# Expert rows of two tiles scaled on ScalarE and summed by accumulating transposes on TensorE, none on VectorE

## The reference

```python
gate = jax.nn.softmax(top_s.astype(jnp.float32), axis=-1).astype(hc.dtype)
u = jnp.take(expert_u, experts, axis=0)
act = jax.nn.gelu(jnp.einsum('chkd,cd->chk', u, hc))
v = jnp.take(expert_v, experts, axis=0)
return jnp.einsum('chk,chkd->cd', gate * act, v)
...
x = x + gate2 * peer(h2, w_query[l], sub_keys_1[l], sub_keys_2[l], expert_u[l], expert_v[l])
return rmsnorm_2(x, final_g)
```

## Time and profile before

| what | value |
|---|---|
| median of three executions | 2421.08 us |
| span of the profiled execution | 2420.9 us |
| TensorE busy in the span | 2179.9 us (90%) |
| VectorE busy | 1680.5 us (69%) |
| ScalarE busy | 742.0 us (31%) |
| first and last gather issued at | 920.7 and 2393.9 us |
| bytes moved | 754.23 MB, of them 588.90 MB by the queue that holds the gathers |

### The profile page before, as it was taken

How to read it: one execution, slowest core, us unless ns; L and a number is a source line. 1 busy time by engine, 2 the same in 40 slices (tenths; PEclk the granted TensorE clock), 3 DMA queues, 4 the chain that set the end, 5 groups by cost and what they waited for, 6 DMA issues and landing times.

```text
span 2420.9 us, 25182 instructions
## 1 busy us (share of the span) xinstructions
PE 2179.9 (90%) x8180; PEld 1438.7 (59%) x8180; DVE 1680.5 (69%) x3748; ACT 742.0 (31%) x2094; POOL 636.1 (26%) x606
## 2 busy tenths in 40 slices
PE   7999998999999998999998999799988977877776
PEld 3444787788888886777774656565444423333332
DVE  5563645476657737889988998877666666676664
ACT  2321345421103212322324223244333333342322
POOL 2100000000110002333334334344444443444342
PEclk9999998999999999999999999899999999999999
DMA  8631020266774348999999999999999999999997
GB/s 344 200 121 54 35 70 1 106 233 222 261 276 146 130 161 322 390 416 398 400 417 419 419 400 384 399 391 420 421 420 421 421 421 421 415 422 421 421 415 306
DMA packets 131785, 754.23 MB, mean 312 GB/s; under 512 B 14544, under 2 KB 14672, under 8 KB 65616
## 3 DMA queue, kind: packets, MB, share of 16 engines
q0 software_dynamic: 87456, 588.90, 60.1%
q1 hardware_dynamic: 44208, 163.84, 18.6%
HBM read 750.59 MB, written 2.10 MB: 311 GB/s over the span
## 4 chain that ended last, share of the span: by engine, by line
PE 52%; DMA 28%; DVE 13%; ACT 4%; issue 2%; POOL 0%; DVEq 0%; SPq 0%; ACTq 0%; POOLq 0%
PE PS L601 51%; DMA arena<-experts_dram,ecur 23%; DVE arena L2605 4%; DVE arena L1874 3%; DMA ring<-down_dram 2%; DVE h_all L1874 2%; DMA ring<-up_dram 1%; ACT const L1756 1%; ACT L1748 1%; DMA ring<-query_dram 1%; ACT arena L1752 1%; DVE h_all L1868 1%; DMA ring<-branch_dram 1%; DVE arena L1868 1%; DMA xT<-x_dram 0%
## 5 line engine op out<-in xcount | busy, mean ns | idle before, releaser
L601 PE MATMUL PS<-arena,const 128*128 128x512 f32 (+2 forms) x1708 | 810.1, 619 | 176.6 <-ACT const L1756 169.8
L601 PE MATMUL PS<-h_all,ring 128*128 128x256 f32 (+2 forms) x3584 | 883.5, 404 | 16.4 <-DMA ring<-up_dram 5.1
L2780 POOL DMA_INDIRECT arena<-experts_dram,ecur x512 | 587.0, 1147 | 1100.1 <-PE PS L601 785.6
L2605 DVE CUSTOM_DVE_ANT_0 arena<-arena 128x1024 f32<-128x1024 f32 x512 | 625.9, 1223 | 278.2 <-DMA arena<-experts_dram,ecur 274.6
L601 PEld LDWEIGHTS PS<-h_all,ring 128*128 128x128 f32 x3584 | 678.9, 191 | 227.7 <-issue 130.8
L601 PEld LDWEIGHTS PS<-arena,const 128*128 128x128 f32 x1708 | 325.1, 197 | 594.1 <-issue 331.9
L1748 ACT ACTIVATE arena<-arena 128x2 f32<-128x2 f32 x255 | 51.6, 202 | 721.4 <-DVE arena L2605 721.0
L601 PE MATMUL PS<-arena,ring 128*128 128x256 f32 x1088 | 245.0, 384 | 7.3 <-DMA ring<-down_dram 4.5
L601 PEld LDWEIGHTS PS<-arena,ring 128*128 128x128 f32 x1088 | 206.4, 192 | 42.7 <-DMA ring<-down_dram 10.7
L601 PE MATMUL PS<-arena 128*128 128x128 f32 (+4 forms) x936 | 137.8, 299 | 8.5 <-DVE arena L1868 3.4
L1756 ACT ACTIVATE const<-const,arena 128x128 f32<-128x128 f32 x415 | 143.5, 387 | 0.0
(11 more groups left out here) (273 smaller groups left out, 1481.2 us busy)
## 6 DMA issues: line engine op xcount, KB each, us to landing
ring<-up_dram SPq DMA_DIRECT2D x88, 512.0 KB, 3.3
ring<-w_in_dram SPq DMA_DIRECT2D x80, 512.0 KB, 4.0
arena<-ada_dram POOLq DMA_DIRECT2D x80, 512.0 KB, 5.5
ring<-w_out_dram SPq DMA_DIRECT2D x32, 512.0 KB, 5.6
ring<-query_dram SPq DMA_DIRECT2D x32, 512.0 KB
ring<-down_dram SPq DMA_DIRECT2D x16, 704.0 KB, 6.3
ring<-branch_dram SPq DMA_DIRECT2D x16, 512.0 KB
arena<-experts_dram,ecur POOLq DMA_INDIRECT x512
```

Of the source, the lines that this page charges most:

```text
L601: return nc.tensor.matmul(o, l, r, start=start, stop=stop)
L2605: V.tensor_tensor_reduce(out=u, in0=u, in1=hrow[:, (r // HEADS) % 2, :], scale=1.0, scalar=0.0, op0=MUL, op1=ADD, accum_out=dots[:, p % NB ...
L2780: nc.gpsimd.indirect_dma_start(out=ring_e[:, g % RING, :], out_offset=None, in_=a["experts"], in_offset=bass.IndirectOffsetOnAxis(ap=ecur[ ...
```

## The change

All 256 rows of tiles 0 and 1 (`turned(p)`, p < 128) now take one other way. ScalarE makes no diagonal; it scales `v` itself in its slot, 1024 columns per row, with the weight as scale (`row_scaled`). TensorE then adds the row with eight transposes of 128 x 128 (`add_turned`) that accumulate into the same two PSUM banks, so that the sum of a tile stands there turned: features on the partitions. No row is summed on VectorE and `side`, `side_row` and `side_sum` are gone; the ring stays at nine slots. At the end of tiles 0 and 1, VectorE adds the turned sum, times the gate, to the turned residual `xT` (`add_tile`, eight instructions of 128 columns at pairs 67 and 131), and `turn_x` turns x with the sum in it, so `finish` drops its two sums of 1024 columns. Tiles 2 and 3 keep diagonals. Four semaphores of an early stage are merged into one, `gate_step`, that counts 1, 2, 3, 4 in the order of the four before.

```diff
-ONE = [*range(1, 48), *range(52, 61), *range(81, 100)]
-BOTH = [*range(4, 46, 4), 14, 18, 19, 22, 23, 30, 34, 38, 39]
-SIDE = sorted([2 * p + 1 for p in ONE] + [2 * p for p in BOTH])
+TURNED = 2
+def turned(p):
+    return p < TURNED * TILE
...
+            def add_turned(row, start, stop):
+                for k in range(KT):
+                    ins = nc.tensor.matmul(PS[:, k // 4, (k % 4) * P:(k % 4 + 1) * P], row[:, k * P:(k + 1) * P], ident,
+                                           start=start and k % 4 == 0, stop=stop and k % 4 == 3, is_transpose=True)
+                return ins
...
             def row_pair(p, start, stop):
-                for k in rows:
-                    r = (p * BATCH + k) % RING
+                for k in range(BATCH):
+                    g = p * BATCH + k
+                    r = g % RING
+                    if turned(p):
+                        pe.wait_ge(row_scaled, g + 1)
+                        add_turned(ring_e[:, r, D:], start and k == 0, stop and k == BATCH - 1).then_inc(rows_used, 1)
+                        continue
...
-            def side_sum(c):
-                pe.wait_ge(side_used, sides(BATCH * TILE * (c + 1)))
-                for v in range(2):
-                    mm(PS[:, v, :], ident, side[:, v * S:(v + 1) * S], False, False)
...
             def weigh_pair(p, r):
-                rows = tensor_rows(p)
-                for k in rows:
+                for k in range(BATCH):
                     act.wait_ge(w_ready2, BATCH * p + k + 1)
-                    A(diag[:, b, k, :], ident, ACT.Copy, scale=wts[:, b, k:k + 1]).then_inc(diag_ready if k == rows[-1] else act_step, 1)
+                    if turned(p):
+                        row = ring_e[:, (BATCH * p + k) % RING, D:]
+                        A(row, row, ACT.Copy, scale=wts[:, b, k:k + 1]).then_inc(row_scaled, 1)
+                    else:
+                        A(diag[:, b, k, :], ident, ACT.Copy, scale=wts[:, b, k:k + 1]).then_inc(diag_ready if k == BATCH - 1 else act_step, 1)
...
+            def add_tile(c):
+                dve.wait_ge(prow_ready, 2 * (c + 1))
+                for k in range(KT):
+                    x = xT[:, k, c * P:(c + 1) * P]
+                    stt(x, prow[:, k * P:(k + 1) * P], mod[:, 1, 40 + k:41 + k], x, MUL, ADD).then_inc(tile_added, 1)
...
                 for j in range(TOPK):
                     g = r * TOPK + j
                     old = g - RING
-                    if old >= 0 and old in SIDE:
-                        pool.wait_ge(side_used, sides(old + 1))
-                    elif old >= 0:
-                        pool.wait_ge(rows_used, by_tensor(old + 1))
+                    if old >= 0:
+                        pool.wait_ge(rows_used, old + 1)
```

More of the change, by code:

```diff
@@ L688, in gate_sums @@
             def gate_sums():
-                pe.wait_ge(g_ready, 1)
+                pe.wait_ge(gate_step, 1)
                 mm(PS[:, 4, 0:16], cst("upper"), gsm[:, 5, :])
-                mm(PS[:, 4, 16:32], ones, gsm[:, 5, :]).then_inc(gc_done, 1)
+                mm(PS[:, 4, 16:32], ones, gsm[:, 5, :]).then_inc(gate_step, 1)
             def decay(h):
@@ L1142, in turn_rows @@
                 ins.then_inc(hr_done, 1)
+            def add_turned(row, start, stop):
[3 more added lines that the diff above has]
+                return ins
             def row_pair(p, start, stop):
-                rows = tensor_rows(p)
-                if rows and p < LAST:
-                    pe.wait_ge(diag_ready, weighed(p + 1))
+                if p < LAST and not turned(p):
+                    pe.wait_ge(diag_ready, p - TURNED * TILE + 1)
                 if start:
@@ L2607, in row_dot @@
                                        ).then_inc(dots_ready, 1)
-            def side_row(g):
-                p, k = divmod(g, BATCH)
-                w = wts[:, p % NB, k:k + 1]
-                row = ring_e[:, g % RING, D:]
-                dve.wait_ge(w_ready2, g + 1)
-                if g == min(q for q in SIDE if q // (BATCH * TILE) == p // TILE):
-                    ts(side, row, w, None, MUL, ALU.bypass).then_inc(side_used, 1)
-                else:
-                    dve.wait_ge(side_used, n.now(side_used))
-                    stt(side, row, w, side, MUL, ADD).then_inc(side_used, 1)
-                n(side_used)
             def finish(c):
@@ L2627, in finish @@
                 dve.wait_ge(brow_ready, 4)
+                if c < TURNED:
+                    V.tensor_tensor_reduce(out=prow, in0=x, in1=x, scale=1.0, scalar=0.0,
+                                           op0=MUL, op1=ADD, accum_out=fin[:, 0:1]).then_inc(fin_sq, 1)
+                    n(fin_sq)
+                    return
                 tt(prow, prow, grow, MUL).then_inc(vec_step, 1)
@@ L2640, in scale_rows @@
                 dve.wait_ge(vec_step, n(vec_step))
-                stt(prow, prow, fin[:, 0:1], frow, MUL, MUL).then_inc(fin_ready, 1)
+                if c < TURNED:
+                    dve.wait_ge(fin_sq, n.now(fin_sq))
+                stt(prow, hrow[:, c % 2, :] if c < TURNED else prow, fin[:, 0:1], frow, MUL, MUL).then_inc(fin_ready, 1)
                 n(fin_ready)
@@ L2668, in beside @@
                 c, q = divmod(p, TILE)
-                for g in range(BATCH * (p - 1), BATCH * p):
-                    if g in SIDE:
-                        side_row(g)
                 for g in range(4):
@@ L2708, in beside @@
                         add_part(m)
+                if c and q == 3 and c <= TURNED:
+                    add_tile(c - 1)
                 if p in FIN_AT:
```

44 lines of the change are left out of this document (18 added, 26 removed).

## The result

| kernel | executions | median, us | range, us | ratio to before, 95% interval |
|---|---|---|---|---|
| before, beside the first runs of the changed one | 4 | 2419.40 | 2417.68 to 2421.54 | 1 |
| changed | 4 | 2433.16 | 2427.31 to 2434.85 | 1.0043 (1.0029 to 1.0057) |
| changed, once more, beside 23 of before (median 2422.07) | 6 | 2431.73 | 2430.79 to 2434.33 | 1.0045 (1.0029 to 1.0061) |

The changed kernel is slower, by 0.43 to 0.45%, some 10.5 us. The forecast was 2419 us and no change. The result is inside the range that was given, 2405 to 2436 us, but it is a loss, and it lies on the rival "TensorE's stalls stay", whose total of 2434 us is close, though, as the profile shows, not by its mechanism.

A forecast was written before the change was run, and what follows sets the result against it. DMA at 420 GB/s was taken as the bound, with TensorE last in pairs 0 to 47 and VectorE in 60 to 79. Terms +2 + 1 - 2.5 - 0.5, then -2, against 2420.9 gave 2419 us; range 2405 to 2436.

The forecast's parts named there:

- TensorE's stalls stay: Rival, pairs 0 to 47: 18 to 29 us of TensorE stalls remain, total about 2434 us; chance 0.22.
- What becomes of the stalls in pairs 0 to 47: Pairs 0 to 47: stalls shrink to 8 us, stretch takes 345 instead of 331 us; net charge 2 us.
- credit behind them, and VectorE's relief: Behind pair 47: DMA runs four or five rows ahead and TensorE catches up, absorbing 12 of the 14 us.
- pairs 64 to 71 with `add_tile`: Pairs 60 to 80: eight `add_tile` instructions, say 2.3 us, against at most one side row less (1.28 us): net +1 us.
- the rest to pair 99: Slots free on time in 1480 to 1500 us win 2.5 us, pair 100's shorter work 0.5 us.
- POOL's waits for side rows: POOL's ten slot waits, 27 us, end with the side rows; less than a tenth counted, -2 us.
- What bounds the kernel: Expert stage: DMA can do 420 GB/s, 29 us lost in all; TensorE comes last in 946 to 1277 us.
- TensorE's price: TensorE, per row: eight transposes at 0.11 us each, 0.88 us, instead of 1.72 us by diagonals.
- 1345 to 1480: Pairs 60 to 79 with the convolution: VectorE stays the limit, windows stay near 404 GB/s, 5 us lost stay.
- 1480 to 1500: Window after the convolution: DMA rises from 355 to over 400 GB/s, 2.5 of 3.1 us won.
- ScalarE: Scaling a row takes 1.15 us; ScalarE has room, at most one row's delay, 2.5 us, in total.
- Clock: Rival: transposes drop TensorE to 1.2 GHz for a tenth of pairs 0 to 47, 17 us more, 2434 us; chance 0.06.

The follow-up runs named there:

- tile 1 alone: Kernel before with only tile 1 changed to scaled rows and transposes; tile 0 keeps diagonals and its 76 side rows: 2421.83 us, ratio 1.0000.
- all side rows: Changed kernel, but VectorE keeps all 95 side rows of before, the other rows still turned on TensorE: 2415.82 us, ratio 0.9978.
- 47 side rows: Changed kernel, but VectorE keeps one side row per pair in pairs 1 to 47 and none behind: 2415.96 us, ratio 0.9963.
- half the transposes: Changed kernel with four of eight transposes per row in pairs 1 to 47, so its sum is incomplete: 2413.37 us, ratio 0.9956.
- 24 late ones: Changed kernel, but VectorE keeps 24 side rows, one per pair in pairs 24 to 47: 2426.91 us, ratio 1.0017.
- tile 0 alone: Kernel before with only tile 0 changed; tile 1 keeps diagonals and its 19 side rows: 2434.50 us, ratio 1.0054.
- scaled twice: Changed kernel with ScalarE scaling each row of pairs 0 to 47 twice, first into an unused buffer: 2432.99 us, ratio 1.0040.
- 24 early ones: Changed kernel, but VectorE keeps 24 side rows, one per pair in pairs 1 to 24: 2420.15 us, ratio 0.9990.
- diagonals only: All rows of tiles 0 and 1 by diagonals on TensorE, none summed on VectorE, none turned: 2520.61 us in one execution.

## Why the prediction was wrong

**The step that failed** is the one under "What becomes of the stalls in pairs 0 to 47": "I charge 14 - 12 = 2 us", with the reason that "the DMA, with time to spare, has nearly all nine landed at the same pair, four or five rows (10 to 12 us) further on". What is ahead of row 95 is bounded by the slots that TensorE frees: a gather whose slot comes free late is issued late, whatever time the transfers have to spare. At row 95, 100 gathers are issued in the changed kernel and 101 in the one before, and in both programs the landed rows end with row 95. The "several rows still to bring" of the prediction were there, but they were there before too, and no further on.

What does come back can be read from rows 95 to 127. With the nine side rows of pairs 52 to 60 this part takes 96.8 and 98.3 us (before), 97.7 (tile 1 alone) and 97.6 (all side rows). Without them, and with TensorE relieved up to row 95, it takes 95.2, 95.3 and 96.8 (47 side rows, half the transposes, 24 late ones): 1.8 less in the mean, which I put down to VectorE's relief. Without them and with TensorE late it takes 93.6 to 94.4 (changed twice, tile 0 alone, scaled twice, 24 early ones): 0.8 to 3.2 less again, 1.8 in the mean. That is the credit: 1 to 3 us where I had 12, and some 5 (90.7) with a TensorE that is 88 us late.

The sum as measured, for the two profiles of the changed kernel against each of the two of before:

| term | predicted, us | against the second profile of before | against the first |
|---|---|---|---|
| pairs 0 to 47 | +14 | +14.6 | +10.3 |
| credit behind them, and VectorE's relief | -12 | -4.6 | -3.1 |
| pairs 64 to 71 with `add_tile` | +1 | +1.8 | +1.8 |
| the rest to pair 99 | -3 | -0.2 to +1.2 | -1.5 to -0.1 |
| POOL's waits for side rows | -2 | not seen as a term | not seen as a term |
| behind pair 99 | 0 | +0.3 | +0.1 |
| sum | -2 | +11.9 to +13.3 | +7.6 to +9.0 |

The third line is rows 127 to 143: 54.3 us in the second profile of before (1368.1 to 1422.4), 56.1 in the second of the changed kernel (1379.0 to 1435.1). All nine profiles with tile 0 turned have 56.0 to 56.2 there, the four others 54.1 to 54.5, so `add_tile` costs nearly its own length. Its eight instructions in the changed kernel's first profile (group; busy, mean ns, idle before):

```profile
L1857 DVE SCALAR_TENSOR_TENSOR xT<-arena,mod,xT 128x128 f32<-128x128 f32 x8 | 2.2, 343 | 0.0
```

The ratio's 10.5 us lie between the two sums, which differ by what one execution of before differs from another. Against either, most of the 12 us is missing. The base of the forecast has a small slip besides: 2420.9 is a span, so it stands for a time of about 2422.6 us and the forecast for 2420.6; against an error of 12 us that is little.

**Point by point.** *What bounds the kernel*: right for 946 to 1277. The 420 GB/s hold in every kernel from 1766 us on (419 to 421). *TensorE's price*: right. The timeline of the changed kernel has sixteen transposes in 1.91 us, here between two weight blocks:

```profile
1003.58 1.91 PE L1127 MATMUL PS<-const,arena 128*128 128x128 f32 x16
```

With 337 us of work and little stall left but the start, the stretch of 344.4 is the predicted 345. *Stalls*: right that they go; TensorE's waits for weights are 0.9 us in the first profile and 1.4 in the second. The rival that kept 18 to 29 us of them is refuted, though its total came out.

*VectorE*: 212 us, as announced (215). *1345 to 1480*: 408 GB/s, near the 404 announced.

*1480 to 1500*: announced over 400, measured 382 and 390, where the two profiles of before have 355 and 372; that is 1 to 2 us (20 x 27/420 and 20 x 18/420) of the 2.5. By rows, 161 to 175 are 1.5 us shorter (first profiles) and 2.3 (second), and rows 175 to 199 are 0.1 us shorter and 3.5 longer, so in the second pair nothing of it is kept. With tile 1 alone the gain goes in the same place, where TensorE is busy 78 of 83 us.

*ScalarE*: its row took 1.134 us, and its length costs nothing; with the row made twice as dear it cost 1.3 us at row 95. The Trainium skill ("ScalarE: Activation LUTs", section "What ACT_TABLE_LOAD costs") gives 280 ns + 0.833 ns a column for an instruction with one operand read per partition. The trace agrees: an estimate of 1133 ns by that formula, 1134 measured.

*Clock*: right, 0.99 in pairs 0 to 47 with 711 transpose records among the matmuls. The clock fell in 1623 to 1766, where TensorE has mostly transposes. The windows of the second profiles of before and of the changed kernel, and of the one with tile 0 alone changed, which has diagonals there:

```profile
1623.00:1766.00 143.00, 131.94 (x396) 72.23 (x395) 98.33 (x250) 59.76 (x182) 56.04 (x53) 0.97 1.01 421
1623.00:1766.00 143.00, 108.49 (x654) 97.86 (x653) 97.82 (x240) 96.47 (x178) 66.12 (x56) 0.86 1.00 412
1623.00:1766.00 143.00, 134.98 (x432) 77.53 (x431) 96.52 (x238) 58.24 (x178) 59.90 (x53) 0.99 1.01 414
```

The first profile of the changed kernel has 0.84 there. The Trainium skill's rule that a transpose doesn't count as activity ("TensorE: Matmul & The Clock Gate", section "Part 4: PE-mode transpose") fits that. It isn't shown by it, because TensorE is also busy for less of the time, 108 us instead of 132; with diagonals and 48 of 60 us busy, in 1480 to 1540, the kernel before had 0.89. No kernel here is seen to have lost time by the clock.

**What the change was.** Two halves that nearly cancel: 95 rows given from VectorE to TensorE cost some 98 us at diagonal prices (one execution of 2520.61 us beside 2422.28); turning the rows took nearly 89 us of it back. The second half is good by itself, with all 95 rows left on VectorE (0.9978) or 47 (0.9963).

**Left open.** The waits of POOL for side rows have no experiment of their own. The late side rows are 0.8 us behind the early ones at row 95, 2.5 at the end of the profiles and 6.8 by the medians. The profiles place 2.4 us of it in rows 95 to 127 (94.4 against 96.8 us) and don't say why. That VectorE's relief, and not another part of pairs 48 to 63, gives 1.8 us is argued from the kernels that share it. Why the two profiles of before stand 4 us apart at row 95 is not known; 23 executions of it spread from 2416.45 to 2428.45 us.

## What to carry to other kernels

When a consumer frees the slots that a transfer needs, a late consumer delays the transfers too: charge the delay nearly in full, and allow no credit for rows that haven't landed at that moment (1 to 3 us here for a delay of 10 to 15). A mean GB/s over a long stretch doesn't say who is the limit, and neither does the issuing engine's wait for slots; whether the consumers wait for rows does, and so do the landed rows at its end. When a change moves work from one engine to another and makes the receiver's unit cheaper in the same step, run the two halves apart. Here 47 rows left on VectorE were enough: they bring TensorE's work (296 us, an estimate) below the 323 us that the fastest kernel took for the stretch, and 67 gained nothing that the times show.

## What the hardware showed that I had not expected

The low clock of a sparse stretch cost nothing that shows. With all side rows kept the profile has the lowest clock of all (0.955) and the kernel is faster than before; rows 199 to 255 took 156.9 us at a clock of 0.86 and at 0.97 alike, with the transfers at 412 and 421 GB/s in that window. Over all profiles but that with diagonals only, rows 199 to 255 take 155.7 to 158.5 us where tile 1 is turned, and 156.3 to 157.4 where it isn't.

Scaling 128x1024 in place on ScalarE, 109 us of it in 344, slowed neither the dot products of VectorE on the same slots (median 1222 ns; 1219 and 1218 in the kernel before, which scales no row in its slot; 1220 where ScalarE scales twice) nor TensorE (a record of 256 columns takes 379 ns in the mean, 383 before).
